# One pass through the second layer's output and query weights for two tiles of tokens, and the samples' last head group moved ahead

## The reference, cut to what matters

```
q, k, v = split(x @ odd_w_in)                  # 1024 x 3072; q and k are rotated by position
o = dilated attention, 16 heads                # samples also read their cached keys and values
x = layer_norm(ALPHA * x + o @ odd_w_out)      # 1024 x 1024
s = (x @ peer_w_q) . sub_keys                  # 1024 x 2048; 8 heads, 2 halves, 128 keys each
slots, gate = the 16 best of each head, softmax of their scores
y = sum over 128 slots: gate * gelu(u[slot] . x) * v[slot]
x = layer_norm(ALPHA * x + y)
```

## Time and profile before

| | us |
|---|---|
| median of 3 runs | 2425.44 (2414.98 to 2430.22) |
| the profiled execution | 2422.81 |
| its span, first to last instruction | 2421.0 |
| PE busy | 1815.2 |
| DVE busy | 1527.2 |
| ACT busy | 557.0 |
| POOL busy | 720.7 |

### The profile page before, as it was taken

The page is one execution under the profiler, slowest core; times in us unless marked ns, Lnnn a source line. Parts: engine busy times, 40 slices in busy tenths (PEclk is TensorE's granted clock), DMA queues, the critical chain, the costliest instruction groups (busy, mean ns, idle before and its releaser), DMA issues.

```text
span 2421.0 us, 18703 instructions
## 1 busy us (share of the span) xinstructions
PE 1815.2 (75%) x5407; PEld 825.2 (34%) x5407; DVE 1527.2 (63%) x3381; ACT 557.0 (23%) x1702; POOL 720.7 (30%) x612
## 2 busy tenths in 40 slices
PE   6895589893978774867867777775778688687765
PEld 4343446432223222434323332332333233223221
DVE  0343441236989556668488598559559875648976
ACT  0101131001232211223133132214213232213222
POOL 4000000001344432333233345333234434434542
PEclk9997556796998996778978999897899899899988
DMA  9211120402989999999999999999799999999997
GB/s 287 66 51 24 36 50 1 174 0 112 421 350 394 421 419 356 363 388 389 414 397 375 413 421 385 411 394 379 281 398 418 397 389 419 409 421 421 406 390 302
DMA packets 146095, 759.20 MB, mean 314 GB/s; under 512 B 22204, under 2 KB 46664, under 8 KB 63944
## 3 DMA queue, kind: packets, MB, share of 16 engines
q0 software_dynamic: 84480, 608.21, 62.2%
q1 hardware_dynamic: 61512, 149.80, 16.7%
HBM read 752.35 MB, written 5.60 MB: 313 GB/s over the span
## 4 chain that ended last, share of the span: by engine, by line
DMA 23%; PE 20%; DVE 19%; issue 5%; SPq 2%; ACT 1%; POOL 1%; PEldq 1%; DVEq 1%; PEld 0%; ACTq 0%
DMA uv<-in_experts_dram,slots 15%; PE ps L1985 11%; DVE uv L1893 6%; PE ps L529 4%; DVE acc L1907 2%; DMA last_w<-in_odd_w_in_dram 2%; DMA first_w<-in_odd_w_in_dram 2%; DMA last_w<-in_peer_w_q_dram 1%; PE ps L878 1%; PE ps L850 1%; PE ps L689 1%; SPq L1597 1%; DVE route_s L1727 1%; PE ps L366 1%; DMA sample_rows<-in_peer_sub_keys_dram 1%
## 5 line engine op out<-in xcount | busy, mean ns | idle before, releaser
L1875 POOL DMA_INDIRECT uv<-in_experts_dram,slots x576 | 690.1, 1198 | 1640.3 <-PE ps L1985 948.1
L1985 PE MATMUL ps<-uv,diag 128*128 128x512 f32 (+1 forms) x1664 | 891.6, 677 | 260.4 <-ACT diag L1961 195.9
L1893 DVE CUSTOM_DVE_ANT_0 uv<-uv,x 128x1024 f32<-128x1024 f32 x512 | 621.9, 1225 | 363.3 <-DMA uv<-in_experts_dram,slots 284.0
L1985 PEld LDWEIGHTS ps<-uv,diag 128*128 128x128 f32 (+1 forms) x1664 | 314.3, 202 | 751.4 <-issue 450.9
L1939 ACT ACTIVATE gelu<-dot 128x2 f32<-128x2 f32 x288 | 58.6, 203 | 1060.3 <-DVE dot L1893 1060.0
L1907 DVE SCALAR_TENSOR_TENSOR acc<-uv,wgt,acc 128x1024 f32<-128x1024 f32 x155 | 198.8, 1282 | 1.4 <-ACT wgt L1948 1.3
L1948 ACT ACTIVATE wgt<-gate,gelu 128x1 f32<-128x1 f32 x576 | 138.1, 287 | 55.7 <-SPq L2088 23.5
L1961 ACT ACTIVATE diag<-const,wgt 128x128 f32<-128x128 f32 (+1 forms) x416 | 148.6, 386 | 9.4
L1893 DVE CUSTOM_DVE_ANT_0 uv<-uv,xs 128x1024 f32<-128x1024 f32 x64 | 78.0, 1225 | 51.3 <-DMA uv<-in_experts_dram,slots 45.6
L445 PE MATMUL ps<-even_w,xT 128*128 128x512 f32 (+3 forms) x240 | 101.1, 569 | 0.0
L529 PE MATMUL ps<-last_w,xT 128*128 128x512 f32 x160 | 77.9, 631 | 18.7 <-DMA last_w<-in_odd_w_in_dram 14.1
(11 more groups left out here) (435 smaller groups left out, 1909.0 us busy)
## 6 DMA issues: line engine op xcount, KB each, us to landing
sample_cache<-in_cache_dil_kv_dram SPq DMA_DIRECT2D x64, 256.0 KB, 9.5
sample_w_in<-in_odd_w_in_dram SPq DMA_DIRECT2D x12, 1024.0 KB, 10.7
first_w<-in_odd_w_in_dram SPq DMA_DIRECT2D x12, 1024.0 KB, 11.5
last_w<-in_odd_w_in_dram SPq DMA_DIRECT2D x12, 1024.0 KB, 13.5
uv<-in_experts_dram,slots POOLq DMA_INDIRECT x576, 10.9
even_w<-in_even_w_in_dram SPq DMA_DIRECT2D x8, 1024.0 KB, 5.8
uv<-in_peer_w_q_dram SPq DMA_DIRECT2D x8, 1024.0 KB, 13.5
late_w<-in_peer_w_q_dram SPq DMA_DIRECT2D x8, 1024.0 KB, 9.3
```

The costliest lines, as they stand in the source:

```text
L1875: self.k.nc.gpsimd.indirect_dma_start(out=self.uv[:, s % RING, :], out_offset=None, in_=self.table, in_offset=bass.IndirectOffsetOnAxis(ap ...
L1893: ins = nc.vector.tensor_tensor_reduce(self.uv[:, s % RING, 0:D], self.uv[:, s % RING, 0:D], x, 1.0, 0.0, ALU.mult, ALU.add, self.dot[:, g ...
L1985: last = nc.tensor.matmul(k.bank(c)[0:m, :], self.diag[:, s % RING, 0:m], self.uv[:, s % RING, D + 512 * c:D + 512 * (c + 1)], start=(j == ...
```

## The change

The samples keep their own attention, but share the second tile's pass through the output weights and through the query weights. `mix_out` takes a list of tiles and is called with (1, 2) in `mixer 1`; the transposes after it cover both. `late_routing_pair` stands in place of two calls of `late_routing`: the sub-keys are loaded and turned once, and the new `project_pair` multiplies each piece of the query weights (1024 columns, two chunks of 128 features, 1 MB) with tile 1 and then with the samples. The samples' last head group, which has to come first, becomes a window of its own from step 278 to 293, in place of "nothing". `mixer 1` runs from step 294 to 369, `route 1 1` from 370 to 405, `route 1 2` from 406 to 465, and nothing from 466 to the end; DVE takes no adds from 370 to 465 and every fourth from 466 on. `mixer 2` is gone.

```
+def project_pair(k, name, w, n, outs, wbuf, tiles, banks):
+    nc, slots, width = k.nc, wbuf.shape[1], 1024
...
+    pieces = [(at, c0) for at in range(0, n, width) for c0 in range(0, KC, 2)]
+    jobs = [(at // 512 + j, which) for at in range(0, n, width) for which in range(2) for j in range(2)]
...
+    stage = Stage(k, 4 * len(pieces) + 1, 1.9)
...
+    @stage.on("sync")
+    def _(sp):
+        for i in range(slots, len(pieces)):
+            sp.wait_ge(piece_done, i - slots + 1)
+            load(sp, i)
...
+        for i, (at, c0) in enumerate(pieces):
+            pe.wait_ge(landed[i % slots], 16 * (i // slots + 1))
+            for which, t in enumerate(tiles):
+                for c in range(2):
+                    for j in range(2):
+                        job = 4 * (at // width) + 2 * which + j
+                        if c0 + c == 0 and job >= len(banks):
+                            pe.wait_ge(copies[job % 2][0], (job - len(banks)) // 2 + 1)
+                        last = nc.tensor.matmul(k.bank(banks[job % len(banks)])[0:ROWS[t], :], k.xT[:, c0 + c, cols(t)],
+                                                wbuf[:, i % slots, width * c + 512 * j:width * c + 512 * (j + 1)],
+                                                start=(c0 + c == 0), stop=(c0 + c == KC - 1), skip_group_check=True)
+                    if which == 1 and c == 1:
+                        last.then_inc(piece_done, 1)
+                    yield
...
     ("route 1 0", FIRST[3] - 48, ()),
-    ("nothing", FIRST[3] - 10, (3,)),
+    ("last group", FIRST[3] - 10, (3,)),
     ("mixer 1", FIRST[3] + 6, (1, 3)),
-    ("route 1 1", FIRST[4] - 48, ()),
-    ("mixer 2", FIRST[4] - 10, (3,)),
-    ("route 1 2", FIRST[5] - 48, ()),
-    ("nothing", FIRST[5] - 10, (3,)),
+    ("route 1 1", FIRST[4] - 46, ()),
+    ("route 1 2", FIRST[4] - 10, ()),
+    ("nothing", FIRST[5] - 78, (3,)),
...
-        stages.append(mix_out(k, name, t, a, w, outer))
-    stages.append(transpose_x(k, name + "_y", tiles, SIDE_BANKS))
+        stages.append(mix_out(k, name, out_tiles, a, w, outer))
+    stages.append(transpose_x(k, name + "_y", out_tiles, SIDE_BANKS))
...
+def last_group(k, name, a, val, kT, qT, cached):
...
+        return sample_groups(k, name, (3,), a, qT, kT, val, cached, outer)
...
+def late_routing_pair(k, name, a, route_tile):
...
+            stages = [turn_keys(k, name + "_keys", a["peer_sub_keys"][1], keys, keysT, SIDE_BANKS),
+                      project_pair(k, name + "_q", a["peer_w_q"][1], 2 * PH * 128,
+                                   (lambda j: rows[:, 512 * j:512 * (j + 1)], lambda j: s_rows[:, 512 * j:512 * (j + 1)]), wbuf, (1, 2),
+                                   SIDE_BANKS),
+                      transposes(k, name + "_qT", groups, SIDE_BANKS)]
...
+            work["mixer 0"] = dilated_tile(k, "first", 0, (0,), a, o, val, kT)
+            late, work["route 1 0"] = late_routing(k, "first", 0, a, r)
+            work["mixer 0"] += late
+            work["last group"] = last_group(k, "sample_b", a, val, kT, s_qT, cached)
+            work["mixer 1"] = dilated_tile(k, "last", 1, (1, 2), a, o, val, kT)
+            late, work["route 1 1"], work["route 1 2"] = late_routing_pair(k, "pair", a, r)
+            work["mixer 1"] += late
```

More of the change, by code:

```diff
@@ L546, in project_wide, with load, _, take_out @@
         stage.on(engine)(lambda eng, side=side: take_out(eng, side, *outs[side]))
+    return stage
+def project_pair(k, name, w, n, outs, wbuf, tiles, banks):
+    nc, slots, width = k.nc, wbuf.shape[1], 1024
+    w_v = w.rearrange("(c p) n -> p c n", p=128)
+    landed = [k.sem(name, f"w_landed{i}") for i in range(slots)]
+    piece_done, v_out, s_out = [k.sem(name, s) for s in ("piece_done", "v_out", "s_out")]
+    pieces = [(at, c0) for at in range(0, n, width) for c0 in range(0, KC, 2)]
+    jobs = [(at // 512 + j, which) for at in range(0, n, width) for which in range(2) for j in range(2)]
+    per = KC // 2
+    stage = Stage(k, 4 * len(pieces) + 1, 1.9)
+    stage.weights[-1] = 0.8
+    copies = [(v_out, nc.vector.tensor_copy), (s_out, nc.scalar.copy)]
+    stage.done = [(v_out, len(jobs) // 2), (s_out, len(jobs) // 2)]
+    def load(sp, i):
+        at, c0 = pieces[i]
+        sp.dma_start(wbuf[:, i % slots, :].rearrange("p (c n) -> p c n", n=width), w_v[:, c0:c0 + 2, at:at + width])\
+          .then_inc(landed[i % slots], 16)
+    @stage.on("early loads")
+    def _(sp):
+        for i in range(slots):
+            load(sp, i)
+    @stage.on("sync")
+    def _(sp):
+        for i in range(slots, len(pieces)):
+            sp.wait_ge(piece_done, i - slots + 1)
+            load(sp, i)
+    @stage.on("tensor")
+    def _(pe):
+        for i, (at, c0) in enumerate(pieces):
[12 more added lines that the diff above has]
+                    yield
+        yield
+    def take_out(eng, side):
+        done, copy = copies[side]
+        for i in range(len(pieces)):
+            if i and i % per == 0:
+                leave(eng, side, i // per - 1)
+            for _ in range(4):
+                yield
+        leave(eng, side, len(pieces) // per - 1)
+        yield
+    def leave(eng, side, group):
+        done, copy = copies[side]
+        for job in range(4 * group + side, 4 * group + 4, 2):
+            j, which = jobs[job]
+            eng.wait_ge(piece_done, per * (group + 1))
+            copy(outs[which](j), k.bank(banks[job % len(banks)])[0:ROWS[tiles[which]], :]).then_inc(done, 1)
+    stage.on("vector")(lambda dve: take_out(dve, 0))
+    stage.on("scalar")(lambda act: take_out(act, 1))
@@ L2092, in _, with dilated_tile @@
             experts.stores(sp)
-def dilated_tile(k, name, t, a, o, val, kT):
+def dilated_tile(k, name, t, out_tiles, a, o, val, kT):
     r, tiles = ROWS[t], (t,)
@@ L2138, in turn_qk, with mix_out @@
     return stage
-def mix_out(k, name, t, a, w, ctx, before_loads=()):
+def mix_out(k, name, tiles, a, w, ctx):
     gb = k.sbuf(name + "_gb", [128, 2, D], ctx=ctx)
@@ L2146, in mix_out @@
     return project_out_and_norm(k, name + "_out", k.xT, lambda i, dst: [(dst, w_v[:, 2 * i:2 * i + 2, :])], a["ln_mix_g"][1],
-                                a["ln_mix_b"][1], w, gb, z, stats, (t,), SIDE_BANKS, before_loads)
+                                a["ln_mix_b"][1], w, gb, z, stats, tiles, SIDE_BANKS)
 def sample_groups(k, name, some, a, qT, kT, val, cached, ctx):
@@ L2176, in samples_first_part @@
     return stages
-def samples_second_part(k, name, a, val, kT, qT, cached):
+def last_group(k, name, a, val, kT, qT, cached):
     with ExitStack() as outer:
[L2184 to L2188, removed]
+        return sample_groups(k, name, (3,), a, qT, kT, val, cached, outer)
+def late_routing_pair(k, name, a, route_tile):
+    with ExitStack() as late:
+        qT = k.sbuf(name + "_qT", [128, 2 * PH, 128], ctx=late)
+        s_qT = k.sbuf(name + "_s_qT", [128, 2 * PH, NS], ctx=late)
+        keysT = k.sbuf(name + "_keysT", [128, 2 * PH, NK], ctx=late)
+        with ExitStack() as load:
+            wbuf = k.sbuf(name + "_w", [128, 3, 2048], ctx=load)
+            rows = k.sbuf(name + "_rows", [128, 2 * PH * 128], ctx=load)
+            s_rows = k.sbuf(name + "_s_rows", [NS, 2 * PH * 128], ctx=load)
+            keys = rows[:, :].rearrange("p (a b) -> p a b", b=128)
+            groups = [([x[:, 128 * (4 * i + j):128 * (4 * i + j + 1)] for j in range(4)], dst[:, 4 * i:4 * i + 4, :])
+                      for x, dst in ((rows, qT), (s_rows, s_qT)) for i in range(4)]
+            stages = [turn_keys(k, name + "_keys", a["peer_sub_keys"][1], keys, keysT, SIDE_BANKS),
[3 more added lines that the diff above has]
+                      transposes(k, name + "_qT", groups, SIDE_BANKS)]
+        with ExitStack() as inner:
+            one = route_tile(1, 1, qT, keysT, inner, own=slice(0, 128))
+        with ExitStack() as inner:
+            return stages, [one], [route_tile(1, 2, s_qT, keysT, inner, own=slice(0, NS))]
 def late_routing(k, name, t, a, route_tile):
```

## The result

The changed kernel takes 2436.65 us (median of 8 runs, 2431.53 to 2445.5), the kernel before, run beside it, 2424.26 us (median of 8). The ratio is 1.0056 with a 95% interval of 1.0036 to 1.0077: some 12 to 14 us more, which lies within the 1% that I named as the limit, inside the range, and 14.7 us above the forecast of 2422 us. It is small, but outside its own uncertainty: the kernel became slower, where I had forecast no change or 2 us less.

The account below looks back on a forecast made before the run. DMA gathers were taken to bound the kernel late, the mixer only partly, with PE, DVE and waits there. Terms -52 + 16 + 38 - 4 = -2 us gave 2422 us, no measurable change, range 2390 to 2456.

Parts of the forecast that it names:

- The bytes: Steps after 406: samples no longer load 14.7 MB of own weights, worth 36 us; 479.1 us to become 427, -52 us.
- the moved: After step 406: 4.2 MB of cached keys and values, 10 us, go to the last head group's new window, not saved.
- The mixer: Second tile's mixer, 76 steps instead of 74, with the samples' projections: +38 us (+5 to +60), to 326 us.
- The query projection: Mixer stage: 64 more matmuls, PE replaces the DMA as the limit, +34 us, to some 83 us.
- The input projection: Mixer stage, full of DMA: 19.3 steps become 15.2 at 2.6 us each, -11 us.
- a second norm in series: Mixer's output projection stage: the samples' norm follows the tile's, adding 10 us within that stage's +25 us.
- The last head group: Steps 278 to 293, before 41.3 us without side work: the samples' group with 16 loads of 256 KB adds +16 us.
- the floor: Last head group's window: the DMA stays full and only the 4.2 MB of loads add time, +10 us.
- the ceiling: Last head group's window: barrier's 12.6 us added undivided, the group's PE work only partly beside the gathers, +29 us.
- The routing: Second tile's routing, 36 steps instead of 38, DVE nearly always busy: -4 us.
- The serial rival: Mixer becomes one serial chain, over some 350 us with DMA share under 0.77: about 2462 us; chance 0.18.
- the faster rival: DMA stays the limit, the mixer's idle PE time takes the new matmuls: about 2386 us; chance 0.21.

## Why the prediction was right or wrong

**The bytes** behaved as worked out: 14.7 MB less on SP's queue, and steps 406 to 575 at 429.2 us against the 427 that I took. Of the -49.9 us the group's removal made 15.1 and the sharing 34.8, against the 10 us that I had for the moved and the 36 us for the saved bytes. Here the DMA share stayed at 0.99 and a step at 2.5 us, so the DMA was the limit before and after. The Trainium skill's figure of about 358 GB/s for loads from HBM ("DMA: Bandwidth & Descriptors", "Where 436 GB/s comes from") isn't the one to price them by: this stretch ran at 409 GB/s.

**The mixer** came out at 325.6 us against 326, its stages at 82.2, 21.5, 72.0, 68.0 and 81.9 us against 76, 22, 71, 74 and 83; PE was busy 243 us in it and not 255. The query projection is the term that carries it, and it held: PE replaces the DMA there, with 80.56 of 81.9 us busy. Leaving out matmuls shortens the mixer by two thirds of the PE time that goes. Two stages are off by 6 us in opposite directions, so some of the closeness of the sum is luck. The input projection gave back 5 us and not 11: with a DMA share of 0.92 it is no longer full of transfers. And the 10 us for a second norm in series was wrong as a reason, since the mixer is as long without it; the stage that it belongs to grew by 19 us and not by 25.

**The last head group** is the step that failed: "I take +16, nearer the floor, because the loads themselves fill the DMA during most of the barrier." It measured +29.9 us, just past the ceiling of +29. The reason given was right as far as it goes. Loads, barrier, key transposes and spread together cost 17.3 us with the DMA at 0.98. What I left at nothing is the group's attention, which I had listed for the ceiling as "the group's own work on PE" and then dropped: 12.6 us, in which the DMA runs short. Where it runs short can be read: from 1522 to 1540 us PE does nothing but scores and expert matmuls, without a pause, DVE stands 10.9 us for those scores with dot products behind them, and the DMA share is 0.61. PE and DVE take side work and expert work in one order, so this wait also holds up the release of gather buffers.

How the 12.6 us divide between PE's own work and the handovers between the engines isn't shown. More steps lower the excess of the window, from 29.9 to 21 us with 24, but the mixer then gives nothing back; fewer expert matmuls were tried only at a lower granted clock. That 16 steps are too few isn't the whole of it either, since the same group took 59.4 us over 16 steps in the samples' window, with its keys loaded ahead and fewer expert matmuls on PE. Those two together weren't tried in steps 278 to 293.

**The routing** gave 2.7 us for a predicted 4.

**The balance.** With that one term at its measured size my sum is -52 + 30 + 38 - 4 = +12, and the medians say +12.4. The frame of the prediction stood: what is saved where the DMA is full is spent again where it isn't. The serial rival's condition, a mixer of over 350 us with a DMA share under 0.77, didn't arise (325.6 us, 0.85), nor did the faster rival's idle PE time take up the new matmuls. Where it was too kind was in treating a window without side work as one with slack. Steps 278 to 293 ran at a DMA share of 0.98 before, so they had no more room for bytes than steps 406 to 575, and the group had fewer of them: in the old place it had some 32 of the 90 steps of `mixer 2` (1926.4 to 2022 us in the trace of before), here 16.

Why eight more steps in the mixer cost 26.1 us, 3.3 us each, stays open: four more steps with adds on PE, of about 1.9 us each, explain 8 us, and the lower granted clock goes with much of the rest. Whether the clock is the cause, or fell because PE waited more, no run separates. No version that does all of the work beat both kernels by more than the measurement tells; the control with adds on DVE in the kernel before, 0.9983, is the nearest to it.

## What to carry to other kernels

Price a saving of bytes together with where its compute lands: a shared pass saves transfers in one place and adds matmuls in another, and it pays only if the place that receives them is not already limited by the engine that runs them. When a chain of dependent pieces is moved between the steps of a pipelined loop, price its work and its waits beside those steps, and not only its bytes; the group that was worth 15 us over some 32 steps cost 30 us over 16. A forecast between a floor and a ceiling needs a reason for each part of the ceiling that it drops, not one reason for the largest part.

## What the hardware showed that I had not expected

The DMA can be full and slower. In the experiment without the group's attention the window with the 16 loads of 256 KB moved 368 GB/s at a share of 0.98; the same steps without the loads moved 394 GB/s at 0.98, and steps 406 to 575 409 GB/s at 0.99. In 58.6 us that is 21.6 MB, which at 394 GB/s would have taken 54.7 us. So some 4 of the 17.3 us of this window, by that estimate, are a lower rate and not bytes. What lowers it no run here separates.
